# Linear attention scores of a head in one stretch, and delta-rule query-key products in column halves

## What is computed

```python
kk = jnp.einsum('bihd,bjhd->bhij', k, k)
...
qk = jnp.einsum('bihd,bjhd->bhij', q, k) * dec
o = (jnp.einsum('bihd,bhdv->bhiv', q, S) * jnp.exp(G)[..., None]
     + jnp.einsum('bhij,bhjv->bhiv', qk, u))
```

```python
att = jnp.einsum('bihd,bjhd,bijhd->bhij', q, k, dec)
o = (jnp.einsum('bihd,bhdv->bihv', q * jnp.exp(cb), S)
     + jnp.einsum('bhij,bjhv->bihv', att, v))
c_last = cb[:, -1]
S_new = (S * jnp.exp(c_last)[..., None]
         + jnp.einsum('bjhd,bjhv->bhdv', k * jnp.exp(c_last[:, None] - cb), v))
```

## Time and profile before

| | us |
|---|---|
| median of three runs | 3279.09 |
| lowest, highest | 3278.41, 3282.0 |
| the profiled execution | 3279.15 |
| its span | 3277.4 |
| PE busy | 3189.0 (97%) |
| DVE, ACT, POOL busy | 1393.1, 1095.6, 462.5 |
| granted TensorE clock, mean | 0.991 |
| linear attention stage | about 2032 to 2870 |
| delta rule stage | about 28 to 860 |

### The profile page before, as it was taken

The page is one execution under the profiler, slowest core; times in us unless marked ns, Lnnn a source line. Parts: engine busy times, 40 slices in busy tenths (PEclk is TensorE's granted clock), DMA queues, the critical chain, the costliest instruction groups (busy, mean ns, idle before and its releaser), DMA issues. The chain is left out here.

```text
span 3277.4 us, 50630 instructions
## 1 busy us (share of the span) xinstructions
PE 3189.0 (97%) x18221; PEld 2391.0 (73%) x18221; DVE 1393.1 (43%) x3381; ACT 1095.6 (33%) x2878; POOL 462.5 (14%) x519
## 2 busy tenths in 40 slices
PE   7999999999799999999999998999999999999999
PEld 5677777776577777776686675888888888777676
DVE  3455555555345555554452134143434333352233
ACT  3344333433144444444201341123333323210341
POOL 1443344433000000000001002000000000011000
PEclk9999999999999999999999999999999999999999
DMA  5211111113421121222442001101111110551101
GB/s 159 74 46 38 36 34 42 40 45 97 106 63 44 47 54 54 55 66 81 153 144 76 15 21 61 52 26 57 50 50 56 44 54 27 171 193 58 39 1 53
DMA packets 256359, 211.78 MB, mean 65 GB/s; under 512 B 29615, under 2 KB 232271, under 8 KB 256167
## 3 DMA queue, kind: packets, MB, share of 16 engines
q1 hardware_dynamic: 250814, 199.53, 21.6%
q10 hardware_dynamic: 5360, 9.67, 0.8%
HBM read 163.19 MB, written 45.99 MB: 64 GB/s over the span
## 5 line engine op out<-in xcount | busy, mean ns | idle before, releaser
L525 PE MATMUL gdn_pj<-hT,Wb 128*128 128x352 f32 x1536 | 515.4, 465 | 10.8 <-ACT gdn_zraw L763 9.2
L525 PEld LDWEIGHTS gdn_pj<-hT,Wb 128*128 128x128 f32 x1536 | 268.9, 192 | 110.7 <-ACT gdn_zraw L763 9.8
L2127 PE MATMUL gla_pj<-gla_TX,gla_S 128*128 128x256 f32 (+1 forms) x736 | 191.2, 393 | 0.0
L2127 PE MATMUL gla_pj<-hT,gla_S 128*128 128x256 f32 (+1 forms) x736 | 187.3, 393 | 0.0
L2127 PEld LDWEIGHTS gla_pj<-hT,gla_S 128*128 128x128 f32 x736 | 139.3, 190 | 26.2
L2127 PEld LDWEIGHTS gla_pj<-gla_TX,gla_S 128*128 128x128 f32 x736 | 138.2, 190 | 26.2
L2127 PE MATMUL band_pj<-hT,Wb 128*128 128x256 f32 x512 | 135.2, 394 | 15.4 <-PEq L45 10.4
L1817 ACT ACTIVATE band_ET<-band_PT 128x512 f32<-128x512 f32 (+2 forms) x144 | 70.5, 490 | 232.0 <-PE band_PX L1643 118.8
L2127 PE MATMUL band_pj<-band_TX,band_S 128*128 128x288 f32 (+1 forms) x512 | 137.3, 398 | 0.0
L2127 PE MATMUL band_pj<-hT,band_S 128*128 128x288 f32 (+1 forms) x512 | 135.8, 398 | 0.0
L3359 PE MATMUL fin_ps<-fin_R,fin_Wx 128*128 128x384 f32 (+1 forms) x384 | 124.7, 468 | 2.2 <-DVE fin_xT L3770 2.1
(11 more groups left out here) (537 smaller groups left out, 6351.0 us busy)
## 6 DMA issues: line engine op xcount, KB each, us to landing
Wb<-in_l_w_in_dram SPq DMA_DIRECT2D x95, 512.0 KB, 8.1
fin_xT<-x_features SPq DMA_DIRECT2D x16, 528.0 KB, 6.8
fin_R<-o_features SPq DMA_DIRECT2D x16, 528.0 KB, 9.8
Wb<-in_l_w_mkv_dram SPq DMA_DIRECT2D x8, 1024.0 KB, 5.6
Wb<-in_l_w_out_dram SPq DMA_DIRECT2D x16, 512.0 KB, 4.2
o_features<-gla_OF ACTq DMA_DIRECT2D x14, 528.0 KB, 7.6
gla_Wv<-in_l_w_in_dram SPq DMA_DIRECT2D x7, 1024.0 KB, 5.4
band_stage<-bias_rows SPq DMA_DIRECT2D x16, 320.0 KB, 8.9
```

Of the source, the lines that this page charges most:

```text
L525: mm = pe.matmul(pj[:, m % 2, 0:w], W[:, j, k, :], hT[:, k, c0:c0 + w], start=k == 0, stop=k == KD - 1)
L2127: mm = pe.matmul(bank[:, 0:w], left(name, k), right(name, k, unit[0], w), start=name in ("P1", "P5", "P2") and k == 0, stop=k == FAST_K - ...
```

## The change

In the linear attention all 27 score products of a head are issued one after the other, group g into bank g of `X` instead of all into bank 0, without waits between them. The transposes follow in three groups with ten steps behind each, also into bank g, and each group waits for `at_ok` of its own group, since it overwrites the scores there. ACT and DVE read the bank g. One matmul of 384 columns into bank 2 is put in front of the stage's first products. In the delta rule each 128x128 query-key product becomes two 64x64 products, one for each chunk, and DVE reads the packed result.

```diff
@@ delta rule, PE
-                            mm = pe.matmul(X3[:, g, 128 * t:128 * t + 128], act3[:, 1, c:c + 128], act3[:, 0, c:c + 128],
-                                           start=True, stop=True)
+                            for a, P in enumerate(HALVES):
+                                c = 384 * g + 128 * t + 64 * a
+                                mm = pe.matmul(X3[P, g, 64 * t:64 * t + 64], act3[:, 1, c:c + 64], act3[:, 0, c:c + 64],
+                                               start=True, stop=True)
@@ delta rule, DVE
-                            mm = dve.tensor_tensor(g3(QK, g)[P, :, P], p3(X3, g)[P, :, P], own(dec, g)[P, :, :], ALU.mult)
+                            mm = dve.tensor_tensor(g3(QK, g)[P, :, P], p3_own(X3, g)[P, :, :], own(dec, g)[P, :, :], ALU.mult)
@@ linear attention, PE
                     for g in range(3):
-                        if g:
-                            pe.wait_ge(at_ok, h * 3 + g)
                         for t in range(3 * g, 3 * g + 3):
...
-                            pe.matmul(X[0:CHUNK, 0, c:c + 64], KK[:, t, 0, :], q[0], start=True, stop=True)
+                            pe.matmul(X[0:CHUNK, g, c:c + 64], KK[:, t, 0, :], q[0], start=True, stop=True)
...
                         mm.then_inc(at_done, 1)
-                        pe.wait_ge(kp_ok, h + 1)
-                        if g:
-                            pe.wait_ge(kt_ok, h * 3 + g)
+                    pe.wait_ge(kp_ok, h + 1)
+                    for g in range(3):
+                        pe.wait_ge(at_ok, h * 3 + g + 1)
                         for t in range(3 * g, 3 * g + 3):
                             c = 128 * (t - 3 * g)
-                            mm = pe.transpose(X[:, 1, c:c + 128], KP[:, cols(t)], ident[:, :])
+                            mm = pe.transpose(X[:, g, c:c + 128], KP[:, cols(t)], ident[:, :])
                         mm.then_inc(kt_done, 1)
                         fill(per_group)
@@ linear attention, PE, start of the stage
+                pe.matmul(X[:, 2, 0:384], ident[:, :], hT[:, 0, 0:384], start=True, stop=True)
                 first_values()
```

More of the change, by code:

```diff
@@ L604, in head @@
                         for t in range(3):
-                            c = 384 * g + 128 * t
-                            mm = pe.matmul(X3[:, g, 128 * t:128 * t + 128], act3[:, 1, c:c + 128], act3[:, 0, c:c + 128],
-                                           start=True, stop=True)
+                            for a, P in enumerate(HALVES):
+                                c = 384 * g + 128 * t + 64 * a
+                                mm = pe.matmul(X3[P, g, 64 * t:64 * t + 64], act3[:, 1, c:c + 64], act3[:, 0, c:c + 64],
+                                               start=True, stop=True)
                         mm.then_inc(qk_done, 1)
@@ L2563, in head @@
                             q = [QG[:, 128 * t + 64 * u:128 * t + 64 * u + 64] for u in range(2)]
-                            pe.matmul(X[0:CHUNK, 0, c:c + 64], KK[:, t, 0, :], q[0], start=True, stop=True)
-                            pe.matmul(X[CHUNK:128, 0, c + 64:c + 128], KK[:, t, 2, :], q[1], start=True, stop=True)
-                            mm = pe.matmul(X[0:CHUNK, 0, c + 64:c + 128], KK[:, t, 1, :], q[1], start=True, stop=True)
+                            pe.matmul(X[0:CHUNK, g, c:c + 64], KK[:, t, 0, :], q[0], start=True, stop=True)
+                            pe.matmul(X[CHUNK:128, g, c + 64:c + 128], KK[:, t, 2, :], q[1], start=True, stop=True)
+                            mm = pe.matmul(X[0:CHUNK, g, c + 64:c + 128], KK[:, t, 1, :], q[1], start=True, stop=True)
                         mm.then_inc(at_done, 1)
-                        pe.wait_ge(kp_ok, h + 1)
-                        if g:
-                            pe.wait_ge(kt_ok, h * 3 + g)
+                    pe.wait_ge(kp_ok, h + 1)
+                    for g in range(3):
+                        pe.wait_ge(at_ok, h * 3 + g + 1)
                         for t in range(3 * g, 3 * g + 3):
                             c = 128 * (t - 3 * g)
-                            mm = pe.transpose(X[:, 1, c:c + 128], KP[:, cols(t)], ident[:, :])
+                            mm = pe.transpose(X[:, g, c:c + 128], KP[:, cols(t)], ident[:, :])
                         mm.then_inc(kt_done, 1)
@@ L2722, in head @@
                         wait(act, p_done, h * TILES)
-                        act.activation(KT[:, 3 * g:3 * g + 3, :], X[:, 1, 0:384].rearrange("p (t n) -> p t n", t=3), ACT.Copy).then_inc(kt_ok, 1)
+                        act.activation(KT[:, 3 * g:3 * g + 3, :], X[:, g, 0:384].rearrange("p (t n) -> p t n", t=3), ACT.Copy).then_inc(kt_ok, 1)
                     for t in range(TILES):
@@ L2850, in head @@
                         dve.wait_ge(at_done, h * 3 + g + 1)
-                        dve.tensor_tensor(AT[:, 3 * g:3 * g + 3, :], X[:, 0, 0:384].rearrange("p (t n) -> p t n", t=3),
+                        dve.tensor_tensor(AT[:, 3 * g:3 * g + 3, :], X[:, g, 0:384].rearrange("p (t n) -> p t n", t=3),
                                           seen[:, :].unsqueeze(1).broadcast_to([128, 3, 128]), ALU.mult).then_inc(at_ok, 1)
```

## The result

| | before | after |
|---|---|---|
| median of 15 runs, us | 3278.41 | 3282.98 |
| lowest, highest | 3274.86, 3282.09 | 3279.51, 3287.47 |
| ratio over all runs | | 1.0017, 95% interval 1.001 to 1.0024 |
| profiled execution, us | 3279.15 | 3285.47 |
| its span | 3277.4 | 3283.8 |

By the ratio, which is estimated over all runs and is not that of the two medians, the change costs 0.17%, some 5.6 us (3.3 to 7.9); the medians differ by 4.6. Forecast was +3.4. The predicted time, 3282.5, is 0.5 us from the median. The cost is real but lies inside the 0.2% that I called no change.

What follows compares the result with a forecast made beforehand. PE, busy 3189.0 of 3277.4 us, was taken as the bound. Round trips -4.7, stall +9.3, halves -1.9 and extra matmul +0.65 give +3.4 on 3279.1, hence 3282.5 us; 8-in-10 range 3275.5 to 3288.

Steps and rivals of the forecast that it cites:

- The saved round trips: Linear-attention scores: one turn to half-width matmuls and back a head instead of three, saving 0.58 us a head, 4.7 in all.
- The new stall: Linear attention, group 2 transposes: PE waits for DVE's step 76 addition, then mask; 1.33 us in seven heads, +9.3 us.
- Rival A: Linear attention: no new stall, mask 2 done before PE wants its bank; 3273.1 us, chance 0.10.
- The halves: Delta rule query-key products as 64x64 pairs: 0.18 us saved a head in heads 0 to 6, 0.6 in head 7; 1.9 us.
- rival B: Delta rule: DVE's chain has slack, so PE's full gain counts, with the stall as forecast; 3279.5 us, chance 0.10.
- Rival C: Delta rule: half-width products do not load weights under running matmuls; 14 us on top, 3296 us, chance 0.03.
- Rival D: Linear attention: seven stalls let the granted clock fall to the 1.2 GHz level; 12 us, 3294 us, chance 0.06.
- The extra matmul: Start of the linear attention: one 384-column matmul plainly added, +0.65 us, up to 1.3 at the 1.2 GHz level.
- The signs I named: Trace changes expected in linear attention and delta rule, such as PE idle before group 2 transposes, about 1.1 us.
- 7 x 0.18 + 0.6: Delta rule: PE gains only what DVE's chain starts earlier in heads 0 to 6, all in head 7; 1.9 us.

Runs made afterwards that it cites:

- e1: Changed kernel, with DVE doing mask 2 of a linear-attention head ahead of the additions of steps 72 and 76: 3274.52 us, 0.9984 of the kernel before.
- e6: Changed kernel, with DVE's mask 2 put between the additions of steps 72 and 76: 3275.74 us, 0.9988 of the kernel before.
- e4: e1, with DVE's subtractions and transposes ahead of its query-key products in the delta rule: 3267.73 us, 0.9965 of the kernel before.
- e5: Kernel before, query-key products whole, with DVE's subtractions and transposes ahead of its query-key products in the delta rule: 3274.67 us, ratio 0.9989.
- e10: Changed kernel with 128 fulfilled waits on PE ahead of head 0 of the delta rule: 3282.58 us, 1.0009 of the kernel before.
- e11: e4 with 128 fulfilled waits on PE ahead of head 0 of the delta rule: 3268.91 us, 0.9969 of the kernel before.
- e7: Kernel before with the extra 384-column matmul sixteen times at the start of the linear attention: 3289.88 us, ratio 1.0032.
- e2: Kernel before with the delta rule's query-key products in halves and nothing else of the change: 3276.4 us, 0.9993 of the kernel before.

## Why the prediction was right

**The saved round trips: right.** 0.58 a head forecast, 0.59 measured in e1 with the stall out of the way.

**The new stall: right in place, number and cause.** It stands at group 2 in seven heads and not in the last. The size was 1.33, measured 1.28. The mask starts 0.09 us before the addition's end (2258.72 against 2258.39 + 0.42), which is the early one of the two ends that I gave. With the slow first transpose on top I had 1.30 to 1.40, so the measured stall lies just below that range, 0.35 us over the seven. Rival A is out for the changed kernel, and e1 and e6 show what it would have looked like: 3274.52 and 3275.74 us, against the 3273.1 worked out for it.

**The halves: right for the heads.** 1.9 forecast, 7 x 0.16 + 0.74 = 1.9 by the trace of the kernel before, 1.5 to 1.9 with the other traces of its code (the last head: 10.85 us from the projection before the products to the one behind L638 before, 10.11 from the same place after). In the last head the chain binds too, a little: the third group of L639 starts at 789.26, 0.15 us behind the end of the tail copy. The term rested on DVE's chain ending last, and rival B on its having slack; e4 and e5 take the chain away and get back 0.74 us and 0.45 us a head, so B falls. One thing I had not looked at: this chain cost the kernel before 0.45 us a head, with no edit to the products at all. In the earlier trace rows it stood there as PE's start 0.15 us behind DVE's end, and I read it only as a limit to the change.

**Rival C, the loads not overlapped: out.** 36 records of L607 in 1.36 us, pairs 0.058 us apart, with loads of 138 ns. The rule of the Trainium skill, TensorE: Matmul & The Clock Gate, Part 3, that a load overlaps only when the row group differs, does not hold for these column halves.

**Rival D, the clock: out.** Seven stalls of 1.1 us by the busy account left the mean granted clock of the stretch at 1.00, the 2.4 GHz level. The mechanism exists in a longer pause: behind the 2.4 us for which PE stands still in e10 and e11 the clock did fall to the 1.2 GHz level, for 3.4 us.

**The extra matmul: 0.65 forecast, 0.66 in e7.** The row I took it from mixes two forms: 256 of its 384 records have 384 columns and 128 have 288, and their busy time over their number isn't the distance of starts. The starts of the 384-column records are 0.323 us apart, so the figure was right, but not by that reading.

**The signs I named.** L2572 idle once in seven heads, about 1.1 us, by DVE: 7.3 us, 7 times. Idle spells before scores 24 to 8: so. PE's busy share down by about 1.3%: 1.1%. A head 0.8 us longer: 0.69. Products 1.4 to 1.6 us: 1.36, just below. Heads of the delta rule shorter by 0.2: 0.16.

**What was missing.** The terms of the sum with their measured sizes give 7 x 1.28 - 8 x 0.59 - 1.9 and between 0.5 and 1.1 for the extra matmul: +2.8 to 3.4 us. The traces show more on top: the gaps in the delta rule, 1.35 and 0.48, and 2 us of pause behind it, hence some 6.7 to 7.3; the runs say 5.6 (3.3 to 7.9). The spans differ by 6.4, but that is no test of the sum, since stretches whose work is the same in both kernels differ by as much: the banded attention by -1.1 us, the first `finish_layer` by +2.1, all that follows the linear attention by -1.6. The forecast was +3.4 on 3279.1; found was +4.6 by the medians on a kernel before that measured 3278.4 this time. The change was 1.2 us larger than forecast and the kernel before 0.7 us faster, so it is partly luck that 3282.5 lies only 0.5 us from 3282.98. My step "7 x 0.18 + 0.6, PE gains what the DVE chain starts earlier" is right for the heads and does not reach the next stage: at its border the last transfer decides, and I had not read that border. e2, the halves alone, is 2.3 us below before all the same (-5.2 to +0.7), so how much of the gaps and the pause there is in an ordinary execution I can't say from one trace of each kernel.

## What to carry to other kernels

When a wait is moved to an engine that is busy all the time, read what stands ahead of the awaited operation in the other engine's order, not how busy that engine is: DVE, at 42%, held PE for 1.28 us a head because one addition of PE's latest product stood ahead of the mask, and moving one mask turned a loss of 0.17% into a gain of 0.16%. A gain inside a stage counts only as far as the border behind it lets it through, so read what starts the next stage, too. Where an engine starts shortly behind another's end, the chain behind that end is worth reordering before the work on the bound engine is made cheaper. Compare the lengths of loop bodies, not the spans of two traces, when the change is a few microseconds.

## What was unexpected of the hardware

A wait whose condition is long fulfilled is not free on PE: 128 in a row held it for 2.4 us, 19 ns each, and of the 0.80 us for which 36 held it, 0.54 reached the head's length. A pause of 2.4 us of PE was followed by 3.4 us at the 1.2 GHz level, which seven pauses of 1.1 us were not. PE's start behind DVE's end was not always the same: the 128x128 transposes start 0.06 us behind the mask's end (2259.33 against 2259.27), and in the delta rule half-width products start 0.15 behind the copy, in heads 0 to 6 of the kernel before; why they differ was not tested. Turning from full to half-width products and back costs up to 0.29 us at 2.4 GHz, measured by leaving two of three turns out: 0.59 us a head in e1, with three waits gone as well. And a single 384-column product behind a gap of 5.9 us ran at 914 ns a record, nearly twice the 490 of its form in `finish_layer`, while sixteen in a row had a mean of 542.
